# Three normalisations and one row scaling in a two-block transformer kernel: chunk-major first tile, rows scaled by column halves

## The reference, cut to what matters

```
# first block, layer i
h  = rmsnorm(x, norm_g[i]) * (1 + scale) + shift
hc = rmsnorm(ctx, norm_g[i]) * (1 + scale_c) + shift_c
x  = x + gate * mixer(h, hc)
# second block, layer i
x = layer_norm(alpha * x + mixer(x), g, b)
x = layer_norm(alpha * x + relu(x @ w_up)**2 @ w_down, g2, b2)
```

## Time and profile before

| what | value |
|---|---|
| timed runs, median (lowest to highest) | 3582.22 us (3577.75 to 3582.32) |
| profiled execution: time | 3576.47 us |
| profiled execution: span | 3574.7 us |
| TensorE busy (PE) | 3467.8 us, 97% of the span |
| VectorE busy (DVE) | 1889.9 us, 53% |
| ScalarE busy (ACT) | 1443.2 us, 40% |
| GpSimd busy (POOL) | 142.8 us, 4% |
| mean granted TensorE clock | 0.99 |
| DMA | 626.07 MB, mean 175 GB/s |

### The profile page before, as it was taken

One profiled execution on the slowest core, in us unless ns is written; L12 is line 12 of the kernel. 1 busy time (PEld: TensorE's weight loads), 2 busy tenths in 40 slices (PEclk: granted clock), 3 DMA queues, 4 the chain that ended last, 5 costly groups with the idle time before them and its releaser, 6 DMA issues.

```text
span 3574.7 us, 43525 instructions
## 1 busy us (share of the span) xinstructions
PE 3467.8 (97%) x18351; PEld 2849.5 (80%) x18351; DVE 1889.9 (53%) x2640; ACT 1443.2 (40%) x1612; POOL 142.8 (4%) x82
## 2 busy tenths in 40 slices
PE   6999999999899999999999999999999999999997
PEld 3677777777887668878888888878998788888886
DVE  3553545532766645457544554464445675445545
ACT  3223334432454543535433443343444444334432
POOL 0000000000000000005000000040000050000000
PEclk9999999999999999999999999999999999999999
DMA  8643333354332265454555555545544455555553
GB/s 343 239 166 140 130 136 123 107 200 177 108 118 95 103 256 187 165 212 160 211 194 189 189 188 191 191 166 188 177 154 164 158 187 212 198 189 188 189 191 127
DMA packets 90782, 626.07 MB, mean 175 GB/s; under 512 B 10326, under 2 KB 11351, under 8 KB 17755
## 3 DMA queue, kind: packets, MB, share of 16 engines
q1 hardware_dynamic: 85472, 606.72, 46.9%
q10 hardware_dynamic: 5116, 16.57, 1.2%
HBM read 621.15 MB, written 2.10 MB: 174 GB/s over the span
## 4 chain that ended last, share of the span: by engine, by line
PE 93%; DVE 3%; ACT 2%; DMA 1%; issue 1%; SPq 0%; DVEq 0%; ACTq 0%
PE PS L584 16%; PE PS L513 14%; PE PS L519 14%; PE PS L514 14%; PE PS L590 8%; PE PS L533 4%; PE PS L540 4%; PE PS L534 4%; PE PS L605 2%; PE PS L615 2%; DMA raw<-in_weights 1%; PE PS L742 1%; PE PS L729 1%; PE PS L885 1%; PE PS L687 1%; PE PS L884 1%
## 5 line engine op out<-in xcount | busy, mean ns | idle before, releaser
L1671 DVE TENSOR_TENSOR wlo<-raw,whi 128x2048 fp32r<-128x2048 f32 (+1 forms) x484 | 1109.7, 2295 | 1145.1 <-ACT whi L1174 1135.0
L1174 ACT ACTIVATE whi<-raw 128x2048 fp32r<-128x2048 f32 (+1 forms) x484 | 911.9, 1886 | 1070.3 <-PE PS L519 613.7
L584 PE MATMUL PS<-xm,whi 128*128 128x512 f32 x2432 | 672.1, 398 | 13.4 <-DVE xm L1687 13.0
L584 PEld LDWEIGHTS PS<-xm,whi 128*128 128x128 f32 x2432 | 419.6, 190 | 72.6 <-DVE xm L1687 9.6
L590 PEld LDWEIGHTS PS<-xm,wlo 128*128 128x128 f32 x2432 | 375.8, 190 | 53.0
L513 PE MATMUL PS<-whi,hid_hi 128*128 128x512 f32 x1024 | 398.7, 389 | 0.0
L514 PE MATMUL PS<-whi,hid_lo 128*128 128x512 f32 x1024 | 398.4, 389 | 0.0
L590 PE MATMUL PS<-xm,wlo 128*128 128x256 f32 x2432 | 389.2, 282 | 0.0
L519 PE MATMUL PS<-wlo,hid_hi 128*128 128x512 f32 x1024 | 273.7, 389 | 0.0
L519 PEld LDWEIGHTS PS<-wlo,hid_hi 128*128 128x128 f32 x1024 | 192.2, 188 | 39.9
L513 PEld LDWEIGHTS PS<-whi,hid_hi 128*128 128x128 f32 x1024 | 192.3, 188 | 39.8
(11 more groups left out here) (336 smaller groups left out, 5085.2 us busy)
## 6 DMA issues: line engine op xcount, KB each, us to landing
raw<-in_weights SPq DMA_DIRECT2D x560, 1024.0 KB, 4.8
lnB<-in_ln ACTq DMA_DIRECT2D x4, 2048.0 KB, 9.5
raw<-in_weights SPq DMA_DIRECT2D x8, 768.0 KB, 4.1
X<-in_x SPq DMA_DIRECT2D x4, 1024.0 KB, 8.4
X<-in_x ACTq DMA_DIRECT2D x4, 1024.0 KB, 15.9
raw<-in_weights SPq DMA_DIRECT2D x8, 512.0 KB, 3.6
raw<-in_weights SPq DMA_DIRECT2D x4, 640.0 KB, 3.8
out_x<-X SPq DMA_DIRECT2D x4, 512.0 KB, 3.4
```

Of the source, the lines that this page charges most:

```text
L584: mm(PS[:, b, :], high_of(n, f), x(4 * k + c).rearrange("p s t -> p (s t)"), start=(k == 0 and c == 0), stop=False, skip_group_check=True)
L1174: return f(dst, src, ACT.Copy)
L1671: v.tensor_tensor(wlo[:, ring.place[n], 0:w], raw[:, ring.place[n], 0:w], whi[:, m % NH, 0:w], ALU.subtract).then_inc(lo_done, 1)
```

## The change

At the first tile of a panel with `row`, `both_panel` now takes each chunk as it arrives for all four blocks: 16 high passes in chunk-major order, then the low passes block by block. The four banks are opened at chunk 0. The other tiles keep their order. In the second layer's row scaling, each of the four instructions is split into two column halves of 1024; the lower halves add to one semaphore and the upper halves to another. `x_pair` waits for the lower at pair 0 and for the upper at pair 4.

```diff
+        xs_ready = [sem(f"xs_ready{u}") for u in range(2)]
...
             def both_panel(key, tiles, x, banks, slot=None, before=None, row=None):
...
+                    by_row = row and k == 0
+                    for c in range(4 if by_row else 0):
+                        row(c)
+                        for ch in range(4):
+                            if c == 0 and ch % 2 == 0:
+                                open_two((*key, ch // 2), banks[ch // 2])
+                            mm(PS[:, banks[ch // 2] + ch % 2, :], high_of(n, slice(c * PW + ch * P, c * PW + (ch + 1) * P)),
+                               x(c).rearrange("p s t -> p (s t)"), start=(c == 0), stop=False, skip_group_check=True)
                     for ch in range(4):
                         u = ch // 2
-                        if k == 0 and ch % 2 == 0:
+                        if k == 0 and ch % 2 == 0 and not by_row:
                             open_two((*key, u), banks[u])
                         b = banks[u] + ch % 2
-                        for c in range(4):
+                        for c in range(0 if by_row else 4):
...
             def x_pair(c):
+                if c % 4 == 0:
+                    pe.wait_ge(xs_ready[c // 4], 4)
...
-            pe.wait_ge(xn_ready, 8)
...
             act.wait_ge(rows_scaled, 1)
-            for t in range(2, 4):
-                f(X[:, t, :], X[:, t, :], ACT.Copy, scale=hrs[:, t:t + 1]).then_inc(xn_ready, 1)
+            for u in range(2):
+                for t in range(2, 4):
+                    x = X[:, t, u * D // 2:(u + 1) * D // 2]
+                    f(x, x, ACT.Copy, scale=hrs[:, t:t + 1]).then_inc(xs_ready[u], 1)
...
-            for t in range(TT):
-                v.tensor_scalar(XN[:, t, :], X[:, t, :], hrs[:, t:t + 1], None, ALU.mult).then_inc(xn_ready, 1)
+            for u in range(2):
+                for t in range(TT):
+                    cols = slice(u * D // 2, (u + 1) * D // 2)
+                    v.tensor_scalar(XN[:, t, cols], X[:, t, cols], hrs[:, t:t + 1], None, ALU.mult).then_inc(xs_ready[u], 1)
```

## The result

The timed runs of the kernel after have a median of 3571.68 us (3566.89 to 3575.42, 16 runs), those of the kernel before, in the same rounds, 3577.51 us (3575.70 to 3584.88, 16 runs). The ratio is 0.9976 with a 95% interval of 0.9969 to 0.9983. That is 0.24% faster, 8.6 us, with an interval of 6 to 11; the medians alone lie 5.8 us apart, the means 7.6, and runs of one kernel differ by some 9. The forecast had 4.7 us, 0.13%, and called 'no difference that can be told' the likeliest outcome. The row scaling went as forecast. At the norms the gain came by another way than the forecast's, that of its rival (a).

What follows compares the result with a forecast made beforehand. TensorE was taken as the bound, at work for 93% of the span. Row scaling 1.15 us plus three norms 3.5 us made 4.7 us off the 3582.22 us median: 3577.5 us, range 3571 to 3582.

Steps and rivals of the forecast that it cites:

- no difference that can be told: Whole kernel: a change below 0.2%, 7.2 us, can't be told from none; this outcome was given 0.72.
- The row scaling: Second layer, first block: column halves let TensorE's transposes start sooner, so the panel starts 1.15 us earlier.
- rival (a): At the norms: TensorE's work before S (chunks 2 and 3 there) raises the clock earlier; 7.5 us in all, 3574.7; chance 0.14.
- What bounds the kernel, and no transfer takes it back: After 914 us: TensorE bounds the kernel and no weight-transfer wait is left, so time saved should reach the end.
- Passes behind S: At each norm, after chunks 2 and 3 arrive (S): eight high passes instead of 14, making the second tile 1.17 us earlier.
- I leave the rise where it is: At the norms: the clock's rise stays S + 5.93 at the first, S + 3.77 at the third; 3.5 us for three.
- the signs that the prediction named for its being wrong: An `xm` wait at tiles 2 to 4, a moved clock rise relative to S, or row-scaling panel under 0.5 us earlier.
- The room behind it: At the norms: later chunks leave room for 2.4, 2.4 and 1.5 us, so 1.17 us at each fits.
- The base of the sum: Whole kernel: 4.7 us is taken from the timed runs' median of 3582.22 us, giving 3577.5.
- Banks: At the norms: alternating banks costs 0, with an upper bound of 19 us, and the banks are no new wait.

Runs made afterwards that it cites:

- rows_only: Kernel before with only the second layer's rows scaled by column halves, the norms as before; ratio 0.9990 (0.9981 to 0.9999) against before.
- Before_fill33: Kernel before, old order of passes, with three useless filler passes ahead of chunk 1 and three ahead of chunks 2 and 3; ratio 0.9991 (0.9980 to 1.0002) against before.
- order_late: Kernel after, new order, but each norm's first pass waits for chunks 2 and 3; one execution, 3581.78 us, with 3575.73 for before beside it.
- all_tiles: Kernel after with the chunk-major order at all four tiles of the first panel after each norm; ratio 0.9968 (0.9957 to 0.9979).
- before_warm: Kernel before, old order, with filler passes in TensorE's idle times around each norm to keep the clock up; ratio 0.9986 (0.9977 to 0.9995) against before.
- after_warm: Kernel after with filler passes (8, 9, 3 and 5) around each norm to keep the clock up; ratio 0.9975 (0.9966 to 0.9985) against before.
- early_split: Kernel after with ACT's third-tile rounding ahead of a norm's first chunk and DVE's low part behind chunks 10 and 11; 3567.32 us, ratio 0.9964 against before.

## Why the prediction was wrong, point by point

**What bounds the kernel, and no transfer takes it back**: right. From the first norm's F to the second's statistics the kernel after takes 689.57 us and rows_only, in which that norm is unchanged, 689.59. (Before's own profile has 689.20.)

**The row scaling**: right, 1.19 us for 1.15. The transposes started 2.36 us behind DVE's first scaling for 2.2 forecast, and ACT modulated at + 4.29 for + 4.2. One sentence there contradicts itself: it has the first context bank only just full at 909.8, and the next paragraph has it full at 908.9. DVE's halves took 0.75 us and were done at + 2.7, so nothing hung on it.

**Passes behind S**: right as counted (eight high passes in place of fourteen, four each at chunks 0 and 1), but not what gave the gain. With the clock held up the two orders have the same F, since the chunks take back the 1.4 us. Before_fill33 against the kernel after, both with the early rise, leaves them 0.3 us at one norm of three. What they would be worth if the chunks came earlier was not run in the old order.

**The step that failed is 'I leave the rise where it is'.** It fixed each norm at 1.17 us, 3.5 in all; measured are 2.44, 2.06 and 1.71, 6.2. The rise moved from 5.9, 6.1 and 3.8 us behind S to 0.9 ahead of it, 1.4 and 1.5 behind it. The fall moved as well, from 5.3, 5.5 and 3.3 us behind the statistics to 5.3, 4.2 and 4.3. No run ties that to the order, and it went with whether the stretch was 3.4 or 6.8 us; what comes back in run after run is that neither is 10.2. Before_fill33 shows that TensorE's being at work ahead of S is enough for that, and order_late that without it the new order gains nothing. I had read the rise at 1619.8, with TensorE busy from S on, as a sign that being busy doesn't hasten it. But the row could not speak of work ahead of S, since there were only two lone passes of 0.8 us. Of the signs that the prediction named for its being wrong, two came: waits for `xm` at tiles 3 and 4, and a rise that moved relative to S.

**The room behind it**: right, and it is what ended the gain. Forecast as cap were 2.4, 2.4 and 1.5 us; counted from S, F fell by 2.45, 2.07 and 1.51 (0.2 of the third norm's 1.71 is that before's chunks came later). I had read them only as safe for 1.17; once the clock was back they were the answer. Rival (a) had this course, 7.5 us for 7.2 measured in the profile's steady part. It was given 0.14. Its full clock from S came true at the first norm alone (first tile done at S + 3.76 for 3.96); at the others the tile took 4.4 us, and only the cap made the sum come out. It also speaks of four rises in the rows, which print three.

**The base of the sum**: 3582.22 us was the median of three runs, and sixteen runs of the same kernel have 3577.51. That the forecast, 3577.5, equals this is chance, and its distance to the measured 3571.68 is not the size of the error; that is the 8.6 us measured for 4.7 forecast.

**Banks**: no cost for changing banks at every pass, as taken; eight passes over four banks take 1.74 us, 0.218 each, against 0.205 within one bank, but a whole tile takes 5.56 us in the new order (all_tiles, second tile of the first norm) and 5.61 in the old. The bank pairs' early opening made no wait either. What the prediction left out is the next panel's banks: at the second norm the fifth tile now waits 0.44 us for them, in either order (before_warm too), so F fell by 2.07 there and not by 2.4. In all_tiles their late closing makes it 1.84.

The Trainium skill's rule ("TensorE: Matmul & The Clock Gate", Part 1), that sustained matmul work lifts the throttle, agrees with these traces: useless passes alone took the low stretch from 10.2 us to 3.4 and 6.8 (before_fill33), and with more of them the clock didn't fall at all (before_warm).

## What to carry to other kernels

Where a profile shows the half clock beside a place where an engine waits in short pieces, price an edit there twice, with the clock's rise as it stands and with it gone, and look for what arrives next; the smaller of the second gain and that room is the likelier answer. Work put into such waits pays through the clock even when it is of no use itself. And a change of some microseconds in 3.5 ms is read from marks inside the profile: where the chunks set them, they agree here to 0.05 us between kernels, and to 0.15 where the clock does at the same length of low stretch, while timed runs of one kernel differ by 9.

## What the runs showed of the hardware that I had not expected

The time from a norm's statistics to its first chunk repeats to 0.05 us in most profiles, and is 0.2 to 0.5 us longer in some (before_fill33, and the third norm of before, rows_only and all_tiles, in the last three of which the clock fell early, 3.1 to 3.3 us behind the statistics). From the first norm's F to the second's statistics it takes 689.57 to 689.59 us in ten of the eleven. The first 900 us differ by 10 us between profiles. DVE's first row scaling starts at 904.72 us in before's profile, 905.14 in after's, 902.74 in after_warm's and 912.88 in early_split's, with no edit ahead of it. The granted clock over the first 100 us has a mean of 0.97, 0.95, 0.97 and 0.88 in these four, in that order. So a later start goes with a lower clock there, where the engines wait for the first weights. Over all eleven profiles the low clock's length ahead of 900 us tells the start: 6.8 us of it go with 902.74, 13.7 with 904.72 and 905.14, 17.1 and 20.5 with 907.8, 23.9 with 909.93 to 911.08, and 27.3 with 912.88. That is about half a us for each us at half clock. Two profiles have one more low stretch behind the row scaling: early_split at 1003 us, of 3.4 us, and before_warm from 1270 to 1280 us (windows):

```profile
1270.00:1280.00 10.00, 9.12 (x31) 4.57 (x33) 2.35 (x8) 3.28 (x7) 0.00 (x0) 0.50 0.19 80
```

And the same stretch of the kernel before:

```profile
1270.00:1280.00 10.00, 10.00 (x63) 4.61 (x64) 4.01 (x15) 3.42 (x8) 0.00 (x0) 1.00 0.51 204
```

It cost 4.2 us: from the panel's first pass to the first norm's statistics before_warm takes 693.73 us and the kernel before 689.55. TensorE waits 2.3 us for DVE just ahead of it, in the kernel before too, where the clock stayed up; thin passes for the modulation vectors stand on both sides. Filling these places and the first 100 us with work wasn't tried.
